# Modulation sums of a two-block transformer kernel: 12 products instead of 48, and loads in four parts

## The reference

```python
ada = (silu(c) @ ada_w + ada_b)            # c: 1024, ada_w: 1024 x 6144
sh1, sc1, g1, sh2, sc2, g2 = split(ada, 6)
u = rms_norm(h, norm1_g) * (1 + sc1) + sh1
z = u @ w_in                                # eight parts of 1024 columns
...                                         # gated linear recurrence (hgrn2), causal convolution
h = h + g1 * (merged @ w_out)
u2 = rms_norm(h, norm2_g) * (1 + sc2) + sh2
h = h + g2 * peer_layer(u2, ...)            # per token 8 x 16 experts' rows are gathered
return rms_norm(h, final_g)
```

## Time and profile before

| | |
|---|---|
| three runs | 1565.99, 1566.13, 1567.95 us (median 1566.13) |
| the profiled execution | 1569.3 us, span 1567.3 us |
| TensorE's mean granted clock | 0.978 |
| PE busy | 1457.9 us, 93% |
| DVE busy | 1051.6 us, 67% |
| ACT busy | 546.1 us, 35% |
| POOL busy | 561.7 us, 36% |
| DMA | 571.91 MB, mean 365 GB/s |
| the adds of `ada_add` | 32, 67.7 us |
| loads of `ada_w` | 32 of 768 KB, median 6.9 us from issue to landing |

### The profile page before, as it was taken

The page is one execution under the profiler, slowest core; times in us unless marked ns, Lnnn a source line. Parts: engine busy times, 40 slices in busy tenths (PEclk is TensorE's granted clock), DMA queues, the critical chain, the costliest instruction groups (busy, mean ns, idle before and its releaser), DMA issues.

```text
span 1567.3 us, 22748 instructions
## 1 busy us (share of the span) xinstructions
PE 1457.9 (93%) x8272; PEld 1120.1 (71%) x8272; DVE 1051.6 (67%) x2170; ACT 546.1 (35%) x1128; POOL 561.7 (36%) x382
## 2 busy tenths in 40 slices
PE   8999999999999999999999999998988978788777
PEld 7999998767999999998989995454444433333333
DVE  6655376876744328998975569775758585858556
ACT  5444354364544436443134252221212121212113
POOL 2455428220344441001002235444544444444441
PEclk9999999999999999999999999999999999989999
DMA  9888968997999998999976959999999999999996
GB/s 363 311 322 326 350 222 328 316 329 252 400 372 369 374 379 296 372 397 342 355 286 226 411 233 426 427 427 427 427 427 427 427 428 427 427 427 427 427 427 261
DMA packets 99814, 571.91 MB, mean 365 GB/s; under 512 B 11536, under 2 KB 11664, under 8 KB 50448
## 3 DMA queue, kind: packets, MB, share of 16 engines
q1 hardware_dynamic: 61056, 298.15, 51.6%
q0 software_dynamic: 37520, 268.47, 40.7%
q10 hardware_dynamic: 1152, 4.16, 0.7%
HBM read 569.67 MB, written 135.27 MB: 450 GB/s over the span
## 4 chain that ended last, share of the span: by engine, by line
PE 65%; DMA 25%; DVE 6%; issue 2%; POOL 2%; ACT 1%; ACTq 0%; DVEq 0%; POOLq 0%
DMA arena<-pairs,eidx 17%; PE ps L2727 9%; PE ps L2113 8%; PE ps L2112 8%; PE ps L2111 8%; DMA ring<-pairs,eidx 6%; PE ps L2504 5%; PE ps L2200 2%; PE ps L2198 2%; PE ps L2199 2%; PE ps L2453 2%; PE ps L2619 2%; PE ps L2520 2%; DVE arena L1965 1%; POOL w_lo L754 1%
## 5 line engine op out<-in xcount | busy, mean ns | idle before, releaser
L2727 PE MATMUL ps<-arena 128*128 128x512 f32 x844 | 398.2, 624 | 66.5 <-ACT arena L1252 66.5
L2727 PEld LDWEIGHTS ps<-arena 128*128 128x128 f32 x844 | 164.9, 199 | 284.8 <-issue 193.9
L1965 DVE CUSTOM_DVE_ANT_0 arena<-arena 128x1024 f32<-128x1024 f32 x211 | 255.0, 1223 | 148.3 <-DMA arena<-pairs,eidx 148.1
L822 POOL DMA_INDIRECT arena<-pairs,eidx x210 | 244.0, 1162 | 254.9 <-PE ps L2727 208.1
L754 POOL TENSOR_TENSOR w_lo<-ring,w_hi 128x1024 fp32r<-128x1024 f32 x76 | 208.0, 2739 | 259.6 <-DVE w_lo L1305 175.7
L2111 PE MATMUL ps<-u_hi,w_hi 128*128 128x256 f32 (+1 forms) x912 | 259.4, 284 | 1.8 <-POOL w_lo L754 1.6
L2113 PE MATMUL ps<-u_hi,w_lo 128*128 128x256 f32 (+1 forms) x912 | 259.5, 285 | 0.0
L2112 PE MATMUL ps<-u_lo,w_hi 128*128 128x256 f32 (+1 forms) x912 | 259.2, 284 | 0.0
L842 ACT ACTIVATE w_hi<-ring 128x1024 fp32r<-128x1024 f32 x188 | 197.8, 1056 | 149.9 <-PE ps L2200 71.2
L2111 PEld LDWEIGHTS ps<-u_hi,w_hi 128*128 128x128 f32 x912 | 172.1, 189 | 3.2 <-issue 2.3
L2113 PEld LDWEIGHTS ps<-u_hi,w_lo 128*128 128x128 f32 x912 | 172.3, 189 | 0.0
(11 more groups left out here) (394 smaller groups left out, 2507.4 us busy)
## 6 DMA issues: line engine op xcount, KB each, us to landing
ring<-in_stream SPq DMA_DIRECT2D x121, 1024.0 KB, 7.2
pairs<-in_peer_u SPq DMA_DIRECT2D x128, 512.0 KB, 7.6
pairs<-in_peer_v SPq DMA_DIRECT2D x128, 512.0 KB, 8.8
arena<-in_ada SPq DMA_DIRECT2D x32, 768.0 KB, 6.9
arena<-in_stream SPq DMA_DIRECT2D x8, 1024.0 KB, 10.3
arena<-pairs,eidx POOLq DMA_INDIRECT x210, 20.4
h<-in_x_t SPq DMA_DIRECT2D x2, 544.0 KB, 5.0
ring<-in_stream SPq DMA_DIRECT2D x2, 512.0 KB, 7.2
```

Of the source, the lines that this page charges most:

```text
L822: pool.indirect_dma_start(slot_of(n), None, pairs, own).then_inc(landing(n)[0], 16)
L1965: dve.tensor_tensor_reduce(row, row, hf[:, n % HEAD_ROWS // TOPK, :], 1.0, 0.0, ALU.mult, ALU.add, dots[:, n % HEAD_ROWS:n % HEAD_ROWS + 1 ...
L2727: mm = pe.matmul(ps[:, Y_BANKS[j // TOPK] + half, :], diag[:, n % DIAGS, :], slot_of(n)[:, D + half * 512:D + half * 512 + 512], start=(hd ...
```

## The change

- The accumulator shrinks to 128 x 1536. Of a tile's place in the ring, each quarter of the partitions (32 rows, `ADA_ROWS`) now holds another quarter of the columns: `load_ada(kt, q)` fetches, for one group of 32 of the 128 matrix rows of `kt`, all four quarters of the columns, each with a transfer of its own of 32 rows x 1536 (192 KB) to its 32 partitions. Each add thus covers 32 rows of the matrix and all 6144 columns, and takes its factors from a `silu_c` of 128 x 32, in which each quarter of partitions holds the same values.
- All adds go to the same accumulator, so each waits for the one before (`q + ADA_Q`).
- `silu_c` is filled by four small transfers behind the stream's piece 3 on SP, and ACT waits for them (`c_in`) ahead of the Silu.
- The sums are 12 products of 128 x 128 x 64 with a new constant `quarter`, whose column g is 1 on the g-th 32 partitions; each gives four columns of sums. They stand once, behind the first piece of ffn2. The 24 in z go.
- DVE adds `ada_b` to all 48 columns and makes both gains in ffn2.
- PE waits for `ada_done` 1 at the second half of piece base + 3, where bank 1 is first written, instead of before piece base + 2; its wait ahead of zi goes, and ACT waits for 3 instead of 4.
- In z, DVE's shifts come behind low parts 4 and 6 (four each), the bounds behind 8, the memset behind 3.

```diff
-        silu_c = sb("silu_c", [P, KT])
+        silu_c = sb("silu_c", [P, KT * ADA_Q])
...
-        ada_acc = view(ADA_Q, ADA_W)
+        ada_acc = view(ADA_Q, ADA_W // ADA_Q)
+        ada_flat = ada_acc.rearrange("p q w -> p (q w)")
+        place(ADA_Q * ADA_W)
...
                 sp.wait_ge(ada_step, kt * ADA_Q + (q + 3))
-                n = kt * ADA_Q + q
-                src = a["ada"][n] if isinstance(n, int) else a["ada"][bass.ds(n, 1)].rearrange("o p w -> p (o w)")
-                sp.dma_start(ada_ring[:, q % 2, :], src).then_inc(ada_in[q % 2], 16)
+                for g in range(ADA_Q):
+                    n = kt * ADA_Q + g
+                    src = a["ada"][n] if isinstance(n, int) else a["ada"][bass.ds(n, 1)].rearrange("o p w -> p (o w)")
+                    own = slice(g * ADA_ROWS, (g + 1) * ADA_ROWS)
+                    sp.dma_start(ada_ring[own, q % 2, :], src[q * ADA_ROWS:(q + 1) * ADA_ROWS, :]).then_inc(ada_in[q % 2], 16)
...
+            c_rows = a["cols"][:, COL["c"]:COL["c"] + KT].rearrange("(q r) k -> r q k", q=ADA_Q)
+            for g in range(ADA_Q):
+                own = silu_c[g * ADA_ROWS:(g + 1) * ADA_ROWS, :].rearrange("r (q k) -> r q k", q=ADA_Q)
+                sp.dma_start(own, c_rows).then_inc(c_in, 16)
...
-                dve.wait_ge(ada_step, kt * ADA_Q + (q + 1))
-                dve.scalar_tensor_tensor(ada_acc[:, q, :], ada_ring[:, q % 2, :], silu_c[:, bass.ds(kt, 1)],
-                                         ada_acc[:, q, :], ALU.mult, ALU.add).then_inc(ada_step, 1)
+                dve.wait_ge(ada_step, kt * ADA_Q + (q + ADA_Q))
+                dve.scalar_tensor_tensor(ada_flat, ada_ring[:, q % 2, :], silu_c[:, bass.ds(q * KT + kt, 1)],
+                                         ada_flat, ALU.mult, ALU.add).then_inc(ada_step, 1)
...
-            dve.wait_ge(ada_mm, 2)
...
-            for k in range(KT):
-                dve.tensor_scalar(u[:, k, 0:SEQ], u[:, k, 0:SEQ], ada[:, k:k + 1], None, ALU.add).then_inc(u_done, 1)
-            then(dve.tensor_tensor(ada[:, 24:48], ps[:, 1, 24:48], V("ada_b", 24, 24), ALU.add), ada_done)
...
                 if n >= 2:
                     z_low(n)
+                if n == 3:
+                    then(dve.memset(pad_glu[:, :, 0:PAD], 0.0), lb_step)
+                if n in (4, 6):
+                    shifted((n - 4) * 2, (n - 4) * 2 + 4)
+                if n == 8:
+                    bounds()
...
-                flat = ada_acc.rearrange("p q w -> p (q w)")
-                for m in range(first, end):
-                    mm = pe.matmul(ps[:, 1, m:m + WIDE], flat[:, m * P:(m + 1) * P], C("ones")[:, 0:WIDE], start=True, stop=True)
+                for j in range(ADA_W // P):
+                    mm = pe.matmul(ps[:, 1, ADA_Q * j:ADA_Q * j + WIDE], ada_flat[:, j * P:(j + 1) * P], C("quarter"), start=True, stop=True)
...
-                    if k and first:
-                        pe.wait_ge(ada_done, 1)
...
+                        if k and e and isinstance(piece, int) and piece == base + 3:
+                            pe.wait_ge(ada_done, 1)
```

More of the change, by code:

```diff
@@ L55 @@
 ADA_W = 6 * D // ADA_Q
+ADA_ROWS = P // ADA_Q
 WIDE = 64
@@ L116 @@
 CONSTS = [("ident", P), ("mean_d", P), ("iota", TOPK), ("mean_256", P), ("mean_128", P), ("mean_64", P), ("mean_96", P),
-          ("ones", P), ("rot", P), ("cos", T), ("sin", T), ("neg_mask", P)]
+          ("ones", P), ("rot", P), ("cos", T), ("sin", T), ("neg_mask", P), ("quarter", WIDE)]
 CON = {}
@@ L155, in constants @@
     put("neg_mask", np.where(np.arange(P)[None, :] > np.arange(P)[:, None], NEG, 0.0).astype(np.float32))
+    quarter = np.zeros((P, ADA_Q), np.float32)
+    quarter[np.arange(P), np.arange(P) // ADA_ROWS] = 1.0
+    put("quarter", quarter)
     put("iota", np.broadcast_to(np.arange(TOPK, dtype=np.float32), (P, TOPK)))
@@ L431, in program @@
         silu_c_done = sem("silu_c_done")
+        c_in = sem("c_in")
         sq_done = sem("sq_done")
@@ L951, in _ @@
             u_high(0)
-            act.activation(silu_c[:, :], V("c", 0, KT), ACT.Silu).then_inc(silu_c_done, 1)
+            act.wait_ge(c_in, 16 * ADA_Q)
+            act.activation(silu_c[:, :], silu_c[:, :], ACT.Silu).then_inc(silu_c_done, 1)
             ffn(0)
@@ L1150, in _ @@
                 late(n)
-            act.wait_ge(ada_done, 4)
+            act.wait_ge(ada_done, 3)
             act.activation(warm, eps[:, :], ACT.Sqrt)
@@ L1367, in ada_add @@
             def ada_add(kt, q):
-                dve.wait_ge(ada_in[q % 2], kt * 32 + (q // 2 * 16 + 16))
-                dve.wait_ge(ada_step, kt * ADA_Q + (q + 1))
-                dve.scalar_tensor_tensor(ada_acc[:, q, :], ada_ring[:, q % 2, :], silu_c[:, bass.ds(kt, 1)],
-                                         ada_acc[:, q, :], ALU.mult, ALU.add).then_inc(ada_step, 1)
+                dve.wait_ge(ada_in[q % 2], (kt * 2 + (q // 2 + 1)) * 16 * ADA_Q)
+                dve.wait_ge(ada_step, kt * ADA_Q + (q + ADA_Q))
+                dve.scalar_tensor_tensor(ada_flat, ada_ring[:, q % 2, :], silu_c[:, bass.ds(q * KT + kt, 1)],
+                                         ada_flat, ALU.mult, ALU.add).then_inc(ada_step, 1)
             def ffn(k, next_gain):
@@ L1572, in _ @@
             dve.wait_ge(ada_mm, 1)
-            then(dve.tensor_tensor(ada[:, 0:24], ps[:, 1, 0:24], V("ada_b", 0, 24), ALU.add), ada_done)
+            by_quarter = "p (q j) -> p q j"
+            sums = ps[:, 1, 0:48].rearrange("p (j q) -> p q j", q=ADA_Q)
+            then(dve.tensor_tensor(ada[:, :].rearrange(by_quarter, q=ADA_Q), sums, V("ada_b", 0, 48).rearrange(by_quarter, q=ADA_Q), ALU.add),
+                 ada_done)
             then(dve.scalar_tensor_tensor(gain1[:, :], ada[:, 8:16], 1.0, V("norm1", 0, KT), ALU.add, ALU.mult), ada_done)
+            then(dve.scalar_tensor_tensor(gain2[:, :], ada[:, 32:40], 1.0, V("norm2", 0, KT), ALU.add, ALU.mult), ada_done)
             ffn(1, lambda k: gain1[:, k:k + 1])
@@ L1596, in _, with shifted, bounds @@
                 dve.tensor_tensor(z_tiles[:, tile, :], ps[:, bank, 0:SEQ], rstd[:, 0:SEQ], ALU.mult).then_inc(z_scaled, 1)
-            for k in range(KT):
-                dve.tensor_scalar(u[:, k, 0:SEQ], u[:, k, 0:SEQ], ada[:, k:k + 1], None, ALU.add).then_inc(u_done, 1)
-            then(dve.tensor_tensor(ada[:, 24:48], ps[:, 1, 24:48], V("ada_b", 24, 24), ALU.add), ada_done)
[L1601 to L1610, removed]
+            def shifted(first, end):
+                for k in range(first, end):
+                    dve.tensor_scalar(u[:, k, 0:SEQ], u[:, k, 0:SEQ], ada[:, k:k + 1], None, ALU.add).then_inc(u_done, 1)
+            def bounds():
+                dve.wait_ge(lb_e, 2)
+                then(dve.tensor_tensor(lb[:, 3], lb[:, 1], lb[:, 2], ALU.add), lb_step)
+                then(dve.reciprocal(lb[:, 4], lb[:, 3]), lb_step)
+                then(dve.tensor_tensor(lb[:, 0], lb[:, 1], lb[:, 4], ALU.mult), lb_step)
+                dve.tensor_scalar(lb[:, 1], lb[:, 0], -1.0, 1.0, ALU.mult, ALU.add).then_inc(lb_done, 1)
             cv = z[:, 0]
@@ L2141, in norm, with ada_sums @@
                     square_mean(n, k)
-            def ada_sums(first, end):
+            def ada_sums():
                 pe.wait_ge(ada_step, KT * ADA_Q + ADA_Q)
-                flat = ada_acc.rearrange("p q w -> p (q w)")
-                for m in range(first, end):
-                    mm = pe.matmul(ps[:, 1, m:m + WIDE], flat[:, m * P:(m + 1) * P], C("ones")[:, 0:WIDE], start=True, stop=True)
+                for j in range(ADA_W // P):
+                    mm = pe.matmul(ps[:, 1, ADA_Q * j:ADA_Q * j + WIDE], ada_flat[:, j * P:(j + 1) * P], C("quarter"), start=True, stop=True)
                 mm.then_inc(ada_mm, 1)
@@ L2165, in up @@
                     for e in range(2):
+                        if k and e and isinstance(piece, int) and piece == base + 3:
+                            assert 2 * slot + e == 1, "the modulation's sums lie in this bank"
+                            pe.wait_ge(ada_done, 1)
                         ready = None
@@ L2173, in up @@
                             if k and e:
-                                ada_sums(0, 24)
+                                ada_sums()
                             elif k == 0 and e == 0:
@@ L2467, in z_piece @@
                                    raw_ready(3) if m + e == 0 else None, (zraw_hi, zraw_lo))
-                        if m + e == 1:
-                            ada_sums(24, 48)
                         continue
@@ L2475, in _ @@
             each_piece(pe, BASE["z"], 16, z_piece, peel=RAW + 1)
-            pe.wait_ge(ada_done, 4)
             for p in range(4):
```

## The result

The changed kernel takes 1599.55 us (median of 4 runs, 1595.47 to 1601.75), against 1567.04 (4 runs) before: ratio 1.0198, 95% interval 1.0183 to 1.0213. The forecast was 1563.2 us, with a range up to 1569.0. The profiled execution has a span of 1599.9 us where it was 1567.3.

The account below looks back on a forecast made before the run. It took PE to bound the kernel, in z only as far as VectorE follows. Gains of 2.64 + 2.54 = 5.2 us less 2.3 us for split loads gave 2.9 us off 1566.13: 1563.2 us, range 1560.0 to 1569.0.

Parts of the forecast that it names:

- ffn1: ... the stream's loads land 7 us and more before their use; free up to that.: In ffn1, slower loads of the matrix cost nothing up to the stream loads' margin of 7 us and more.
- x: All loads of the matrix: extra time a load in four parts takes to land; from 0 to 3.9 us.
- Near 208 us: Two adds side by side, now chained: 0.1 us lost; the second load lands 1.5 us before use.
- x = 1.4: All split loads: the value taken, from a load sharing its queue, 5.6 us to land against 4.2 alone.
- Projections: Three chained loads make the last add 1.46 us later, against 1.4 us of slack: 0.1 us lost.
- the forecast's cover: In w_out, the low part of ffn2's first piece is ready 2.1 us early; of 4.2 us, 2.1 are lost.
- rival B: All split loads: a part's data moves at half the rate, x = 2.1, 7.1 us lost, 1568.0 us; chance 0.28.
- Issues: Loads in four parts: 128 transfers instead of 32, 0.33 us an issue; losses at x = 1.4 sum to 2.3 us.
- The sums in ffn2, 2.64 us: Behind ffn2's first piece, 12 products instead of 24 save PE 2.64 us, VectorE's cover being just enough; bounds 2.4 and 2.64.
- The sums in z, 2.54 us, held by VectorE: In z, 5.27 us of sums go, but VectorE lets PE come only 2.54 us earlier; bounds 1.9 and 5.27.
- the gap of PE behind VectorE that the forecast named as its sign: In z, PE idle before a piece near 638 us by some 2.7 us in all, released by VectorE's low part.
- the 0.66 us of lead behind the bounds: In z, VectorE runs 0.66 us ahead of before once its bounds are done; with 1.88 of cover, 2.54 us.

Follow-up runs that it names:

- split loads alone: The kernel before with each load of the matrix in four transfers of 32 neighbouring rows, nothing else changed: 1595.79 us, ratio 1.0173.
- spread rows: The kernel before with each load in four transfers of 32 rows, each to every fourth partition: 1572.22 us, ratio 1.0021.
- columns: The kernel before with each load in four transfers of 128 rows x 384 columns: 1571.71 us, ratio 1.0020.
- the old order: The kernel with early exponentials, with VectorE's shifts, bounds and memset back in front of low part 2 of z: 1564.86 us, ratio 0.9980.
- the kernel with early exponentials: The changed kernel with each load one transfer of 128 rows, and ScalarE's two exponentials moved from z to the end of attention: 1561.34 us, ratio 0.9961.

## Why the prediction was wrong, point by point

- **"ffn1: ... the stream's loads land 7 us and more before their use; free up to that."** This step failed. It treated x as a delay of one load that a margin hides. But x is work of the queues: 2.0 us for each load, 16 times in ffn1. The idle time of the queues, which has to take it, is 0.10 x 12.1 = 1.2 us in a period; the rest eats the margin, which is gone at 87 us, and then everything behind in the queue is late. With split loads alone (1.6 us a load) the margin held, but the queues were full all the same and the loads at the end of ffn1 landed late. The row that showed this was in the profile of before, the DMA share of 0.90 in ffn1 (0.85 in the projections), and the sum never used it.
- **"Near 208 us ... x = 1.4 is hidden", "Projections: ... 0.1 us is lost."** Here the cost landed: 16.5 and 13.3 us of PE's waiting, for the queue's backlog and for loads that take 10 to 14 us from the first part's issue to the last part's landing, instead of 6 to 7.4. At 208 us x was 17 us in the changed kernel (24.2 for 7.1) and 8 with split loads alone. The loads were priced from a queue with room, and the tile was the wrong one: the forecast watched what PE takes at L2300 of before, with 1.4 us of slack, but PE stopped at an earlier one, at L2291 of before (L2314 after). VectorE had it ready at 277.04 and PE took it at 281.00, so its 4.0 us of cover were gone too.
- **x = 1.4.** In w_out, where nothing else is in the queue, it was near: parts issued 0.5 us apart land 0.85 us apart, the last 5.4 us after the first issue, where a whole load took 4.2: x = 1.2. The adds there waited 9.4 us (6.8 before), and PE waited for the low part that was the forecast's cover 2.2 us where the forecast said 2.1 (the stage as a whole grew by 0.8 us only, as its granted clock was 1.00 and not 0.94 as in the profile of before). The sentence that no transfer of the trace of before goes to fewer than 128 partitions is wrong: GpSimd issues 16 of about 1 KB to one partition each (L776 and L777), 5.9 us to landing; they are too small to price x. The row of the wait:

```profile
PE ps L2149 <- DVE w_lo L1319: 2.2, 1, 2.2
```

  The mechanism was rival B's, half the rate; at 0.28 it stood behind the forecast, and its own sum (1568.0) missed the same term: it priced the 2.1 us as a delay of each load, and not as 32 x 2.1 us taken from queues that were 0.90 full.
- **Issues.** The number of transfers by itself, which the forecast priced at 2.3 us, costs 2 to 3 us (spread rows 1.0021, columns 1.0020). The size was about right, for the case that didn't come.
- **The sums in ffn2, 2.64 us.** Right: the 24 passes take 2.60 us, to the next product (5.28), and the stage is 2.5 us shorter. The two gains and the wider sum on VectorE cost no PE time.

```profile
445.62 2.79 PE L2170 MATMUL ps<-con,arena 128*128 128x64 f32 x24
448.22 0.36 PE L2134 MATMUL ps<-raw_hi,w_hi 128*128 128x256 f32 x1
```

- **The sums in z, 2.54 us, held by VectorE.** 1.5 us came, and the gap of PE behind VectorE that the forecast named as its sign did not. Of VectorE's waits the one for the tile came as priced (1.4 us) and the one for a high part nearly so (0.37, forecast 0.45); the 0.66 us of lead behind the bounds is 0.57 by the forecast's own terms (3.55 - 1.09 - 1.09 - 0.80). The new order does what it should: PE's wait for VectorE is 2.6 us with the old order and 0.2 with the new, once ScalarE is out of the way. But ScalarE was named only as VectorE's supplier; the tile that starts at 619.28 also frees PE's bank. In the changed kernel:

```profile
PE ps L2134 <- ACT arena L1073: 2.0, 1, 2.0
```

  With that wait gone the z stage gives 4.0 us, more than the 2.54, since VectorE's own wait for this tile (1.4 us, which I had subtracted) falls to 0.3 us with it. Of the 5.2 us of gains forecast 4.0 came (2.5 in ffn2, 1.5 in z); of the miss of 36 us nearly all is the loads.

## What to carry to other kernels

Price a slower transfer as work of the queue first, times its number, against the queue's idle share in each stage, and only then as a delay against a margin. Here transfers to 32 or 64 neighbouring partitions cost 1.6 to 2.0 us more queue time for a load that took 2.0 spread over all; if a layout needs parts, lay the data out in memory so that one transfer of 128 rows brings them all, or give each part every fourth partition. When work is taken from the engine that leads, list every engine that hands it something in that stretch: the next wait was for ScalarE, behind its table load, and where the clock fell after it (in three of five profiles) that cost almost as much again.

## What the runs showed of the hardware

- 0.79 MB in four transfers to 32 neighbouring partitions, or two to 64, take 1.6 to 2.0 us more of the 16 engines' time, over the whole queue, than in one of 128; in four to every fourth partition, nothing measurable (809 and 810 us in all). Their own packets took 3.2 to 3.4 us a load instead of 2.0 (2.1 when spread); most of the rest stands in the packets of other loads in the queue.
- After the same idle time of PE of 2.03 us in z the granted clock fell from 1.00 to 0.50 for 3.4 us in three profiles and stayed at 1.00 in two; after the wait of 0.5 us in the kernel with early exponentials it stayed at 1.00.
- Single parts of 192 KB to 32 neighbouring partitions, issued 0.5 us apart into a queue with nothing else, landed 0.85 us apart, one behind another.
